# Blockwise transposes on VectorE, with their blocks moved inside SBUF, in place of transposes on TensorE

## What is computed

```python
for layer in range(2):
    h = rms_norm(x, norm_w[layer])
    z = h @ w_in                                  # 4096 x 13312 (AB) or 4096 x 10240 (C)
    # A: q, k = rope(rms_norm(q)), rope(rms_norm(k))
    p = softmax(q @ k.T * scale + bias)           # per head: 256 x 256
    y = concat(p @ v) * silu(gate)                # per head: 256 x 128
    x = x + y @ w_out                             # 4096 x 4096
out = rms_norm(x, final_norm_w)
```

## Time and profile before

| | |
|---|---|
| median of 3 runs | 2896.82 us (2896.24 to 2897.06) |
| profiled execution, its time | 2896.34 us |
| its span (first to last instruction) | 2894.2 us |
| granted clock of TensorE | 0.998 |
| busy: PE, DVE, ACT, POOL | 2877.5, 1609.0, 1346.5, 15.5 us |
| DMA | 554.30 MB, mean 192 GB/s |

### The profile page before, as it was taken

One profiled execution on the slowest core, in us unless ns is written; L12 is line 12 of the kernel. 1 busy time (PEld: TensorE's weight loads), 2 busy tenths in 40 slices (PEclk: granted clock), 3 DMA queues, 4 the chain that ended last, 5 costly groups with the idle time before them and its releaser, 6 DMA issues.

```text
span 2894.2 us, 38403 instructions
## 1 busy us (share of the span) xinstructions
PE 2877.5 (99%) x13313; PEld 2389.8 (83%) x13313; DVE 1609.0 (56%) x1934; ACT 1346.5 (47%) x1740; POOL 15.5 (1%) x14
## 2 busy tenths in 40 slices
PE   9999999999999999999999999999999999999998
PEld 7888888888888888888888888888888888888887
DVE  7655666545545455455555445556554655565554
ACT  5444455444444444444444444545544455443333
POOL 0000000000000000000000000000000000000000
PEclk9999999999999999999999999999999999999999
DMA  9665665566666665666666666555666556576665
GB/s 331 190 186 171 174 178 169 175 189 193 180 201 176 189 197 175 198 195 218 218 202 209 199 194 181 168 177 170 181 176 193 170 170 179 169 263 192 193 192 181
DMA packets 287112, 554.30 MB, mean 192 GB/s; under 512 B 17552, under 2 KB 22800, under 8 KB 286992
## 3 DMA queue, kind: packets, MB, share of 16 engines
q1 hardware_dynamic: 286704, 552.14, 62.9%
q10 hardware_dynamic: 288, 0.52, 0.1%
HBM read 544.21 MB, written 8.39 MB: 191 GB/s over the span
## 4 chain that ended last, share of the span: by engine, by line
PE 98%; DVE 1%; issue 0%; DMA 0%; ACT 0%; SPq 0%; POOLq 0%; POOL 0%; DVEq 0%; ACTq 0%
PE proj L979 31%; PE proj L981 31%; PE proj L980 31%; PE tr_ps L1073 1%; PE x_ps L1049 1%; PE o_ps L981 1%; PE o_ps L980 1%; PE sc_ps L981 1%; PE o_ps L979 1%; PE sc_ps L980 1%; PE sc_ps L979 1%; PE o_ps L1083 0%; DMA xT<-in_x_cols 0%; DVE w_lo L670 0%; DVE swap L757 0%
## 5 line engine op out<-in xcount | busy, mean ns | idle before, releaser
L670 DVE TENSOR_TENSOR w_lo<-raw,w_hi 128x1024 fp32r<-128x1024 f32 x990 | 1212.3, 1225 | 1120.6 <-ACT w_hi L554 1113.8
L554 ACT ACTIVATE w_hi<-raw 128x1024 fp32r<-128x1024 f32 x990 | 1048.0, 1059 | 935.0 <-PE proj L981 797.4
L979 PE MATMUL proj<-w_hi,h_hi 128*128 128x512 f32 x2940 | 1162.5, 395 | 4.3 <-DVE w_lo L706 3.8
L981 PE MATMUL proj<-w_hi,h_lo 128*128 128x512 f32 x2940 | 1147.4, 390 | 0.0
L980 PE MATMUL proj<-w_lo,h_hi 128*128 128x512 f32 x2940 | 1145.7, 390 | 0.0
L981 PEld LDWEIGHTS proj<-w_hi,h_lo 128*128 128x128 f32 x2940 | 552.1, 188 | 118.5
L979 PEld LDWEIGHTS proj<-w_hi,h_hi 128*128 128x128 f32 x2940 | 552.7, 188 | 113.5 <-DVE w_lo L706 4.2
L980 PEld LDWEIGHTS proj<-w_lo,h_hi 128*128 128x128 f32 x2940 | 553.4, 188 | 108.5
L979 PE MATMUL proj<-w_hi,y_hi 128*128 128x512 f32 x1024 | 401.5, 392 | 0.0
L981 PE MATMUL proj<-w_hi,y_lo 128*128 128x512 f32 x1024 | 398.9, 390 | 0.0
L980 PE MATMUL proj<-w_lo,y_hi 128*128 128x512 f32 x1024 | 398.6, 389 | 0.0
(11 more groups left out here) (118 smaller groups left out, 1105.7 us busy)
## 6 DMA issues: line engine op xcount, KB each, us to landing
raw<-in_w_in_ab SPq DMA_DIRECT2D x415, 512.0 KB, 3.7
raw<-in_w_in_c SPq DMA_DIRECT2D x320, 512.0 KB, 4.1
raw<-in_w_out_ab SPq DMA_DIRECT2D x128, 512.0 KB, 3.7
raw<-in_w_out_c SPq DMA_DIRECT2D x128, 512.0 KB, 4.0
x_in<-in_x SPq DMA_DIRECT2D x8, 512.0 KB, 6.9
bias<-in_bias_b SPq DMA_DIRECT2D x16, 256.0 KB, 3.7
x_fin<-x_residual SPq DMA_DIRECT2D x4, 1024.0 KB, 7.8
xT<-in_x_cols SPq DMA_DIRECT2D x6, 512.0 KB, 6.5
```

The lines of the kernel that those rows point to most:

```text
L554: nc.scalar.activation(w_hi[:, slot], raw[:, slot], ACT.Copy).then_inc(hi_ready, 1)
L670: nc.vector.tensor_tensor(w_lo[:, slot], raw[:, slot], w_hi[:, slot].bitcast(F32), ALU.subtract) \
L979: nc.tensor.matmul(dst, hi, r_hi, start=start, stop=False)
L981: return nc.tensor.matmul(dst, lo, r_hi, start=False, stop=stop)
```

## The change

The transposes on PE are gone. DVE transposes each 32x32 block in place (`nc.vector.transpose`), writing a staging tile in which the blocks that belong to one group of 32 target partitions are next to each other: [128, 4, x, 32]. Then 16 DMAs inside SBUF move 4 x 4 block columns, each from 32 partitions to 32 partitions. SP issues the eight for q = 0 and 1, ACT the eight for q = 2 and 3. `x` is 8 for a turn of q, k or h (1 KB per partition and DMA) and 6 for a head (probabilities and gate together, 768 bytes per partition). ACT and DVE then split the landed tile as before, from SBUF.

Steps: q, k and h are turned in steps 0, 3 or 4 (`TURN_AT`) by one DVE instruction of 128x1024 and split four steps later; on side A and for k_norm the heads start one step later (8 instead of 7). In a head DVE turns the probabilities and the scaled gate two steps after the scores (`TO_TURN`), ACT rounds in the fifth step (`TO_HI`), DVE makes the low part in the sixth, PE multiplies with v in the sixth, in the middle of a block (`values`), y is made in the seventh and its rest in the eighth. SP does its puts five steps later in its own list (`SP_LEAD`), behind the load of that step. DVE now does rope, turns and attention before `w_lo` in its step, and ACT splits a landed turn before `w_hi`. There is one buffer for the bias instead of two, and `y`, the landing and the staging tiles share memory with others. The load of `ident` falls away.

```diff
-Q_ROUNDS = {"A": (5, 6), "C": (3, 4)}
-BQ_ROUNDS, BK_ROUNDS = (1, 2), (3, 4)
-HEAD_STEP = {"A": 7, "B": 5, "C": 5}
+TURN_AT = {"k_norm": (3,), "A": (3,), "k": (0,), "C": (0,), "qk": (0, 4), "h": (0, 4)}
+SP_LEAD = 5
+SP_PARTS, ACT_PARTS = (0, 1), (2, 3)
+SPLIT_AFTER = 4
+HEAD_STEP = {"A": 8, "B": 5, "C": 5}
 HEAD_GAP = 5
-TO_PROBS, TO_PT, TO_GT, TO_PV, TO_Y, TO_REST = 1, 3, 4, 5, 6, 7
-H_STEPS = (2, 4, 6, 8)
+TO_PROBS, TO_TURN, TO_HI, TO_PT, TO_PV, TO_Y, TO_REST = 1, 2, 5, 6, 6, 7, 8
...
+            def put_head(p, i):
+
+                sp.wait_ge(head_turned, p.batch * HB + i + 1)
+                for q in SP_PARTS:
+                    for j in range(NQ):
+                        sp.dma_start(head_land[j * QB:(j + 1) * QB, q], head_stage[q * QB:(q + 1) * QB, j]) \
+                            .then_inc(head_in[0], 16)
...
+                    for k in turns_at(p, b - SP_LEAD):
+                        put_turn(p, k)
+                    if p.side in ("A", "B", "C"):
+                        i = head_at(p, b, TO_TURN + SP_LEAD)
+                        if i is not None:
+                            put_head(p, i)
...
+                    for k in turns_at(p, b):
+                        act.wait_ge(turned, p.x0 + k + 1)
+                        for q in ACT_PARTS:
+                            for j in range(NQ):
+                                nc.scalar.dma_start(landing[j * QB:(j + 1) * QB, q],
+                                                    turn_tiles(p, k)[1][q * QB:(q + 1) * QB, j]).then_inc(turn_in[1], 16)
...
+                i = head_at(p, b, TO_TURN)
                 if i is not None:
                     h = p.batch * HB + i
-                    act.wait_ge(pt_filled, h + 1)
-                    nc.scalar.activation(probsT_hi[:], tr_ps[:], ACT.Copy).then_inc(pt_hi_ready, 1)
-                i = head_at(p, b, TO_GT)
+                    act.wait_ge(head_turned, h + 1)
+                    for q in ACT_PARTS:
+                        for j in range(NQ):
+                            nc.scalar.dma_start(head_land[j * QB:(j + 1) * QB, q], head_stage[q * QB:(q + 1) * QB, j]) \
+                                .then_inc(head_in[1], 16)
+                i = head_at(p, b, TO_HI)
                 if i is not None:
                     h = p.batch * HB + i
-                    act.wait_ge(gt_filled, h + 1)
-                    if p.batch0 > 0 or i > 0:
-                        act.wait_ge(y_split, h)
-                    nc.scalar.activation(y[:], o_ps[:, 1], ACT.Copy).then_inc(gt_ready, 1)
+                    for half in head_in:
+                        act.wait_ge(half, 16 * NQ * 2 * (h + 1))
+                    nc.scalar.activation(headT_hi[:, :, :2 * TT], head_land[:, :, :2 * TT], ACT.Copy) \
+                        .then_inc(pt_hi_ready, 1)
...
+                    columns = head_stage[:].rearrange("p j x r -> p x j r")
+                    nc.vector.transpose(columns[:, :2 * TT], probs[:].rearrange("p t (k j r) -> p (t k) j r", k=TT, j=NQ))
                     dve.wait_ge(inverses, inverses_after(p.side, h))
...
+                    dve.wait_ge(gate_scaled, h + 1)
+                    nc.vector.transpose(columns[:, 2 * TT:], zb[:, :, i * HD:(i + 1) * HD].rearrange("p t (j r) -> p t j r", j=NQ)) \
+                        .then_inc(head_turned, 1)
...
+            def turn(p, k):
+
+                source, stage, _, _ = turn_tiles(p, k)
+                if p.side in ("A", "k_norm"):
+                    dve.wait_ge(roped, ROPE_STEPS * (1 if p.side == "k_norm" else p.batch + 2))
+                else:
+                    dve.wait_ge(drained[k], 2 * p.n)
+                nc.vector.transpose(stage[:].rearrange("p j x r -> p x j r"),
+                                    source[:].rearrange("p t (h j r) -> p (t h) j r", h=HB, j=NQ)).then_inc(turned, 1)
...
                 for j, t in [(j, t) for j in range(2) for t in range(TT)]:
+                    if (j, t) == (1, 0) and p.side in ("A", "B", "C"):
+                        values(p, b)
...
-            def heads_round(p, k, src, i):
-
-                if isinstance(p.x0, int) and p.x0 + k == 0:
-                    pe.wait_ge(ident_loaded, 16)
-                if not (isinstance(p.x0, int) and p.x0 + k == 0):
-                    pe.wait_ge(x_drained, p.x0 + k)
-                for j in range(2):
-                    for t in range(TT):
-                        d = (2 * i + j) * HD
-                        last = nc.tensor.transpose(x_ps[:, j, t * P:(t + 1) * P], src[:, t, d:d + HD], ident[:])
-                last.then_inc(x_filled, 1)
```

More of the change, by code:

```diff
@@ L119, in __init__ @@
         self.batch0, self.x_batch0, self.v0 = batch, x_batch, v
-        self.x_uses = {"none": 0, "k_norm": 2, "k": 2, "A": 2, "B": 0, "C": 2, "qk": 4, "h": 4}[side]
+        self.x_uses = {"none": 0, "k_norm": 1, "k": 1, "A": 1, "B": 0, "C": 1, "qk": 2, "h": 2}[side]
     def at(self, i):
@@ L199, in kv_head, with turns_at @@
     return {"A": p.batch, "B": None, "C": p.batch - (8 if p.batch0 < 12 else 12)}[p.side]
[L202 to L210, removed]
+def turns_at(p, b):
+    return [k for k, step in enumerate(TURN_AT.get(p.side, ())) if step == b]
 def ahead(p, b):
@@ L580, in body @@
                 for b in range(NB):
+                    for k in turns_at(p, b - SPLIT_AFTER):
+                        _, _, hi, _ = turn_tiles(p, k)
+                        for half in turn_in:
+                            act.wait_ge(half, 16 * NQ * 2 * (p.x0 + k + 1))
+                        if p.side == "h":
+                            for m in range(HB):
+                                c = (p.x_batch0 + p.i) * 8 + k * HB + m
+                                last = nc.scalar.activation(
+                                    h_hi[:, bass.ds(c, 1)].rearrange("p a (t q r) -> p (a t) q r", t=TT, q=NQ),
+                                    by_tokens(landing[:, :, m::HB]), ACT.Copy, scale=norm_w[:, 1, bass.ds(c, 1)])
+                        else:
+                            last = nc.scalar.activation(hi[:].rearrange("p x (q r) -> p x q r", q=NQ),
+                                                        landing[:].rearrange("p q x r -> p x q r"), ACT.Copy)
+                        last.then_inc(x_hi, 1)
                     split_hi_at(p, b)
@@ new lines, in split_turn @@
+            def split_turn(p, k):
+                _, _, hi, lo = turn_tiles(p, k)
+                dve.wait_ge(x_hi, p.x0 + k + 1)
+                if p.side == "h":
+                    for m in range(HB):
+                        c = (p.x_batch0 + p.i) * 8 + k * HB + m
+                        for t in range(TT):
+                            chunk = lambda tile: tile[:, bass.ds(c, 1), t * P:(t + 1) * P] \
+                                .rearrange("p a (q r) -> p (a q) r", q=NQ)
+                            last = nc.vector.scalar_tensor_tensor(chunk(h_lo), landing[:, :, t * HB + m],
+                                                                  norm_w[:, 1, bass.ds(c, 1)], chunk(h_hi).bitcast(F32),
+                                                                  ALU.mult, ALU.subtract)
+                else:
+                    rows = lambda tile: tile[:].rearrange("p x (q r) -> p x q r", q=NQ)
+                    last = nc.vector.tensor_tensor(rows(lo), landing[:].rearrange("p q x r -> p x q r"),
+                                                   rows(hi).bitcast(F32), ALU.subtract)
+                last.then_inc(x_split, 1)
@@ L884, in body @@
                 for b in range(NB):
+                    if p.side == "k_norm":
+                        if b == 0:
+                            dve.wait_ge(drained[0], 2 * p.n)
+                        rope(b, cos_k, sin_k, 0, True)
+                    if p.side == "A":
+                        if b == 0:
+                            dve.wait_ge(drained[0], 2 * p.n)
+                        rope(b, cos_q, sin_q, p.batch + 1, False)
+                    for k in turns_at(p, b - SPLIT_AFTER):
+                        split_turn(p, k)
+                    for k in turns_at(p, b):
+                        turn(p, k)
+                    if p.side in ("A", "B", "C"):
+                        finish_y(p, b)
+                        if p.side == "C" and p.batch0 == 8 and b == 0:
+                            dve.wait_ge(dist_loaded, 16)
+                        attend(p, b)
                     split_lo(p, b)
@@ L938, in body @@
                             nc.vector.memset(sq_sum[:], 0.0).then_inc(summed, 1)
-                    if p.side in ("A", "B", "C"):
-                        if p.side == "C" and p.batch0 == 8 and b == 0:
-                            dve.wait_ge(dist_loaded, 16)
-                        attend(p, b)
             walk(dve, body)
```

217 lines of the change are left out of this document (89 added, 128 removed).

## The result

The changed kernel takes 2944.43 us (median of 4 runs, 2942.16 to 2945.74) against 2896.94 for the kernel before on the same chip (4 runs, 2896.24 to 2897.37): a ratio of 1.0163, 95% interval 1.0146 to 1.0181. The change costs 47.5 us where I forecast a gain of 71.

The account below looks back on a forecast made before the run. PE, busy 99%, was taken to bound the kernel: 2894.2 - 78 for removed transposes + 4.0 + 2.3 + 0.9 for boundary stalls gave a span of 2823.4 us, so a time of 2826, range 2815 to 2845 (chance 0.60).

Parts of the forecast that it names:

- the price of an issue: ACT's sequencer, eight transfers per head: 0.46 us each, 3.7 us in all, bounds 0.40 and 0.94.
- the point of loss: Issue price at which the period passes 16.2 us and the change becomes a loss: 0.66 us per issue.
- The ring of a head: C heads, from values to values through ACT and DVE: 14.6 us against PE's period of 15.08.
- its spare: Margin by which the loop of a C head closes within PE's period: 0.5 us.
- closes late, moderately: Rival for the heads: C heads stall about 0.6 us, total near 2860 us; chance 0.19.
- The boundaries: Between pairs, ACT's issues uncovered: stalls 4.0 us at C, 2.3 at k_norm, 0.9 at A, nothing at qk, h, k.
- The C boundaries: Eight C pairs, ACT issuing only after the silu drain: PE stalls 0.5 us each, together 4.0.
- The gain on PE: Transposes removed from PE's list: 47.4 us in heads and 30.5 in rounds for q, k and h, in all 78.
- reading runs of 32 elements: PE's score and value passes, runs of 32 instead of 512: priced at nothing; 9 us if it cost 10%.
- The landing: A head's small transfers: near 2.3 us to land, covered by 3.9 us before ACT's copy of the probabilities.
- The packets: DMA engines: 48,640 new packets, adding 11 points to 63% busy if each were as long as one of 2 KB.
- The two queues hold each other up: Rival: ACT and SP take turns, 0.92 us an issue, ring 18.3 us, total near 3065 us; chance 0.10.

Follow-up runs that it names:

- e11: e4, with ACT issuing nine sets of eight transfers after its last store while SP is idle, to time an issue: 2876.38 us (one run).
- e10: e4, with 8 extra stores to a DRAM tensor nobody reads, issued by ACT at every head and turn: 2877.74 us.
- e6: The changed kernel, but head blocks go through DRAM as in e4; turns of q, k and h stay as changed: 2886.81 us.
- e7: The changed kernel, but turns of q, k and h go through DRAM as in e4; heads stay as changed: 2886.65 us.
- e4: The changed kernel, but blocks go through DRAM: SP stores in one transfer and loads back in four, ACT issues nothing: 2823.78 us.
- e12: e4, with 1 extra store to a DRAM tensor nobody reads, issued by ACT at every head and turn: 2825.03 us.
- e5: The changed kernel, but in C heads SP issues its eight transfers two steps later, after ACT's: 3058.45 us (one run).
- e9: The changed kernel, with ACT's eight issues split into 4 and, one step and one w_hi later, 4: 2931.22 us.

## Why the prediction was wrong

**The step that failed** is the price of an issue: "I take 0.46, so 3.7 us for eight." Measured: 0.61 each, 0.64 from start to start, and 0.2 more for one of the eight: 5.2 us. The bounds, 0.40 and 0.94, held it. The 0.46 came from two loads out of DRAM, and e11 shows that it is right for those (0.44 to 0.45); I carried it over to transfers inside SBUF, of which the kernel before had none. A price without a row of its own needed the middle of its bounds, 0.67, and that was already beyond the 0.66 that the prediction itself had named as the point of loss.

**The ring of a head.** Terms of the earlier trace rows held: turns 0.69 and 0.45 (0.69 and 0.42 taken), 1.25 for 1024 columns; PE alone 15.07 (15.08). The parts beside the issues were 11.5 where I had 14.6 - 3.7 = 10.9: three w_lo take 3.92 and not 3.75, and 0.24 us pass before the bias step. These two make 0.4; the other 0.2 has no known place. With eight issues of 3.9 us e10 gave third heads at 15.35. So the count of the ring was 0.6 short, more than its spare of 0.5, and the issues added 1.5.

**The rival "closes late, moderately"** had the mechanism and was too mild: "At 0.6 per issue C heads stall about 0.6 us". The second and third of a batch stall 0.6 and 1.7 us, third heads of A and B 0.4 and 1.1, and with the last head of each batch e6 puts the heads at 57.6 us where that rival had 19 and a few more on B.

**The boundaries** were the second step to fail, on their own account. I had 7.2 us in all and nothing for qk, h and k ("no silu, at least 0.9 spare"). e7 measures 57.8. PE paused 4.7 us after k_norm (2.3 forecast), 2.0 to 3.6 at A (0.3), 2.5 at k, 1.5 at qk and 3.3 to 3.7 at h. Part is the price of an issue, but e10, with 4.2 to 5.8 us for eight, still paused 3.9 after k_norm, 1.4 to 2.4 at A and 2.3 to 2.7 at h. I had looked at what ACT does after the turn and not at how long it waits for it: nothing was added for what DVE does ahead of the turn at h, nor for the w_hi that stand behind ACT's wait.

The C boundaries, for which I had the most (0.5 each, 4.0 together), went the other way: PE paused at two of the eight, for 0.9 and 0.7 us. I had let ACT's issues start behind the silu drain. They start beside it:

```profile
1991.21 0.69 ACT L603 ACTIVATE zb<-proj,rms 128x512 f32<-128x512 f32 x1 [0.16 <-PE proj L1056]
1991.30 0.51 ACTq L650 DMA_DIRECT2D landing<-q_stage  x1
...
1991.84 4.57 ACTq L650 DMA_DIRECT2D landing<-q_stage  x7
1996.51 1.06 ACT L591 ACTIVATE w_hi<-raw 128x1024 fp32r<-128x1024 f32 x1 [4.03 <-issue]
```

The two that paused are those in which one issue took 1.8 and 1.5 us, with a long one on SP at the same time (2.1 and 1.2). Ten of ACT's bursts in the changed kernel have such an issue, also those after k_norm, before the first A batch (the pause of 3.6) and at k; the runs don't tell what it waits for.

**The clock** was no term of the sum at all. Nine of the eleven pauses of 1.9 us or more were followed by a stretch at 1.2 GHz, together 17 us more than before.

**What each error was worth.** With the issues at 0.44 to 0.48, e10's 2877.7 would have been within the range, and the sign right. This is an approximation: e10 uses DRAM, and its eight stores took 3.9 us in a head but 4.7 in the median at a turn. By it 2944.4 - 2877.7 = 67 us are the price of an issue, and 2877.7 - 2826 = 52 us the boundaries, the clock, the ring's 0.6 and the late load of the last batch.

**What held.** The gain on PE: e4 and e12, with ACT free, are 72 and 71 us faster, against 78 less small pauses, so reading runs of 32 elements costs PE nothing that shows (passes of scores and values start 0.120 us apart before and after). The landing: 1.8 to 1.9 us, below the 2.3 taken, and covered. The packets were more than estimated, q1 and q10 together 72,816 above the kernel before (the earlier trace rows has its q1; q10 had 288) and not 48,640, some 48 for each small transfer; nothing hung on it.

**"The two queues hold each other up"** is refuted at the size that the rival gave it, 0.92 us an issue: the median is 612 ns with SP beside ACT, after it or idle (e5, e11). What is left of it is 0.2 us in one issue of a burst. The Trainium skill (Perfetto Trace Analysis, DMA Instruction - HWDGE) has two sequencers share the generator under a lock; by that rule ACT's issues would become shorter without SP's. In e5 one of the eight does, from 0.82 to 0.61 us, and the other seven don't.

**Coalescing.** e4 puts 5 transfers where there were 16, and gains 120.6 us. The Trainium skill (DMA: Bandwidth & Descriptors, Rules for kernel authors) asks for this, because small transfers pay mostly overhead; the rule is right here, but the overhead that was paid did not lie in flight: landing was covered, and the time of the engine that issued was not.

**Left open:** why an issue inside SBUF costs 0.17 us more; what the single long issues wait for; why the clock stayed up behind two of the long pauses; and whether the blocks could be moved within SBUF by fewer transfers, which wasn't tried.

## What to carry to other kernels

Count a transfer as work of the engine that issues it, 0.61 us inside SBUF and 0.44 to or from DRAM in this kernel, and put bursts on an engine whose next work nobody waits for. When an engine waits for a signal ahead of a burst, add the wait to the burst and compare both with the stock of finished blocks downstream (here, by the estimate above, some 6.5 us of ACT). Where a price has no row of its own, use the middle of its bounds and look at the sign there.

## What was not expected of the hardware

- The issue inside SBUF takes 612 ns on ACT and 590 on SP, whatever the bytes (128 or 768) and partitions (32 or 128: 622); the same burst to or from DRAM takes 442 to 454. The first of a burst is mostly quicker, 514 to 532 and 309 to 352 (but 618 and 1223 in two sets of e11).
- With both queues starting a burst inside SBUF at the same moment, only ACT's second issue is longer, 0.82 us instead of 0.61. In ten bursts of the changed kernel one issue took 1.1 to 2.1 us on ACT and about as long on SP at the same time.
- A route with more steps can be the cheaper one: out to DRAM and back takes 6.0 us from the first issue to the last landing (2030.66 to 2036.62 in a C head of e4), where the 16 direct transfers take 6.5 (4.6 to the last issue, 1.9 to its landing), and it leaves ACT free.
- Small transfers issued behind a 512 KB load in flight landed late in e9, after 3.5 us in the median instead of 1.9; in the head shown they landed with the load, after 3.8 and 4.5.
- Nine of eleven pauses of PE of 1.9 us or more inside the changed kernel were followed by a granted clock of 1.2 GHz for 3.4 to 6.8 us; not those of 2.5 us at 611 and of 3.35 at 1447. None of the shorter ones (1.6 us and less) was.
